# A down projection in seven products for eight, with its splits shared by GpSimd and VectorE

## The reference, cut to what matters

```python
def ffn_sublayer(x, g_pre, w_up_l, w_down_l, g_post):
    h = rmsnorm(x, g_pre)
    a = jax.nn.relu(jnp.einsum('btd,df->btf', h, w_up_l))
    return x + rmsnorm(jnp.einsum('btf,fd->btd', a * a, w_down_l), g_post)
```

## Time and profile before

| | |
|---|---|
| median of 3 runs | 2623.96 us (2621.02 to 2625.25) |
| span of the profiled execution | 2616.5 us |
| PE busy | 2570.5 us, 98% |
| POOL busy | 1296.8 us, 50% |
| ACT busy | 934.8 us, 36% |
| DVE busy | 761.8 us, 29% |

### The profile page before, as it was taken

The page is one execution under the profiler, slowest core; times in us unless marked ns, Lnnn a source line. Parts: engine busy times, 40 slices in busy tenths (PEclk is TensorE's granted clock), DMA queues, the critical chain, the costliest instruction groups (busy, mean ns, idle before and its releaser), DMA issues.

```text
span 2616.5 us, 34806 instructions
## 1 busy us (share of the span) xinstructions
PE 2570.5 (98%) x13946; PEld 2226.2 (85%) x13946; DVE 761.8 (29%) x1667; ACT 934.8 (36%) x1594; POOL 1296.8 (50%) x832
## 2 busy tenths in 40 slices
PE   7999999999999999999999999999999999999998
PEld 6899999999996467788888888878888878898997
DVE  6431111266663225311112111232111234112114
ACT  4001110087775534432234223253323244332232
POOL 1210000067762565855556567476567365654553
PEclk9999999999999999999999999999999999999999
DMA  5312314289977954543345354355454253532332
GB/s 185 113 41 67 109 59 121 69 174 191 172 141 205 297 172 153 193 145 129 113 145 194 129 173 145 112 178 176 149 175 145 98 178 126 171 130 92 131 129 89
DMA packets 264105, 373.72 MB, mean 143 GB/s; under 512 B 78677, under 2 KB 199069, under 8 KB 259033
## 3 DMA queue, kind: packets, MB, share of 16 engines
q1 hardware_dynamic: 243410, 263.37, 35.4%
q10 hardware_dynamic: 14518, 89.43, 9.5%
q0 software_dynamic: 6016, 18.68, 2.5%
HBM read 323.39 MB, written 103.76 MB: 163 GB/s over the span
## 4 chain that ended last, share of the span: by engine, by line
PE 91%; POOL 2%; DVE 2%; ACT 1%; issue 1%; DMA 1%; SPq 0%; ACTq 0%; DVEq 0%; POOLq 0%
PE ml_y L1911 31%; PE ml_up L1869 8%; PE ml_up L1871 8%; PE ml_up L1870 8%; PE pj_acc L481 6%; PE pj_acc L483 6%; PE pj_acc L482 6%; PE at_o L1150 5%; PE at_turn L1130 3%; PE at_score L1119 2%; PE at_score L1120 1%; PE de_s L2574 1%; POOL ml_w_lo L1784 1%; PE de_kt L2555 1%; PE ml_y L1906 1%
## 5 line engine op out<-in xcount | busy, mean ns | idle before, releaser
L1784 POOL TENSOR_TENSOR ml_w_lo<-em_raw,ml_w_hi 128x1024 fp32r<-128x1024 f32 x288 | 700.9, 2435 | 449.3 <-ACT ml_w_hi L1956 449.3
L1956 ACT CAST ml_w_hi<-em_raw 128x1024 fp32r<-128x1024 f32 x288 | 301.7, 1048 | 546.5 <-PE ml_y L1911 353.0
L1911 PE MATMUL ml_y<-ml_w_hi,ml_a_hi 128*128 128x512 f32 x1216 | 475.9, 391 | 3.3 <-POOL ml_w_lo L1784 3.3
L1911 PE MATMUL ml_y<-ml_w_hi,ml_a_lo 128*128 128x512 f32 x1216 | 473.4, 389 | 0.0
L1911 PE MATMUL ml_y<-ml_w_lo,ml_a_hi 128*128 128x512 f32 x1216 | 473.4, 389 | 0.0
L1869 PE MATMUL ml_up<-ml_h_hi,ml_w_hi 128*128 128x512 f32 (+1 forms) x1280 | 450.0, 352 | 1.9 <-POOL ml_w_lo L1784 1.9
L1871 PE MATMUL ml_up<-ml_h_hi,ml_w_lo 128*128 128x512 f32 (+1 forms) x1280 | 449.7, 351 | 0.0
L1870 PE MATMUL ml_up<-ml_h_lo,ml_w_hi 128*128 128x512 f32 (+1 forms) x1280 | 449.6, 351 | 0.0
L481 PE MATMUL pj_acc<-pj_h_hi,pj_w_hi 128*128 128x424 f32 (+1 forms) x800 | 290.0, 363 | 5.8 <-DVE pj_h_lo L699 5.8
L482 PE MATMUL pj_acc<-pj_h_lo,pj_w_hi 128*128 128x424 f32 (+1 forms) x800 | 283.2, 354 | 0.0
L483 PE MATMUL pj_acc<-pj_h_hi,pj_w_lo 128*128 128x424 f32 (+1 forms) x800 | 283.2, 354 | 0.0
(11 more groups left out here) (274 smaller groups left out, 3342.4 us busy)
## 6 DMA issues: line engine op xcount, KB each, us to landing
em_raw<-in_w_up SPq DMA_DIRECT2D x64, 1024.0 KB, 5.3
em_raw<-in_w_down SPq DMA_DIRECT2D x64, 1024.0 KB, 5.1
out_o_a_k_s<-in_cache_a_k ACTq DMA_DIRECT2D x8, 3060.0 KB, 12.6
out_o_a_v_s<-in_cache_a_v ACTq DMA_DIRECT2D x8, 3060.0 KB, 12.1
em_raw<-scratch_pt SPq DMA_DIRECT2D x34, 512.0 KB, 7.0
em_raw<-in_w_out SPq DMA_DIRECT2D x16, 1024.0 KB, 5.0
scratch_pt<-pj_proj SPq DMA_DIRECT2D x10, 1056.0 KB, 4.1
pj_w<-in_w_in SPq DMA_DIRECT2D x20, 512.0 KB, 3.9
```

The costliest lines, as they stand in the source:

```text
L1784: nc.gpsimd.tensor_tensor(split_of(w_lo, n), raw_of(n), f32(split_of(w_hi, n)), ALU.subtract).then_inc(w_lo_ready, 1)
L1911: last = pe.matmul(out, p[:, f, t0:t0 + m], w[:, b, :], start=(f == 0 and p is act_hi and w is hi), stop=(f == PF - 1 and p is act_lo))
L1956: nc.scalar.copy(split_of(w_hi, n), raw_of(n)).then_inc(w_hi_ready, 1)
```

## The change

**Seven products for eight.** The hidden blocks of a part are now four (`PARTS` is 8, not 4), and a part's down projection is seen as a product of 2x2 blocks: the rows are the token tiles 0, 1 (one half, 256 tokens) and 2, 3 (the other), the inner halves are two hidden blocks each, and the columns are the two halves of D. A Strassen scheme computes it with seven products, called P1, P7, P2, P6, P5, P3, P4 in their order, in place of eight. Each has 12 matmuls (two token tiles, two inner blocks, three per product). Sums of activations (`first_sums`, `second_sums`: four per part, L2403) and of weights (`w_sum`: four per part, in place in `em_raw`, L2448) come first, on DVE. P2 is accumulated onto the bank of P1, P3 onto P5, P4 onto P7, each after DVE has read the bank. Three products go straight to the output tile, P1 and P6 into an extra tile `ml_shared` that is added at the end of a group (`share`). The 64 samples keep the ordinary product: 16 matmuls a part in P1, P7, P2 and P3, which is as many as before.

**Who splits.** POOL keeps the `w_lo` of P1, P7, P2 and P6 and of the op units; DVE makes the `w_lo` of the up units and of P5, P3 and P4 (L2454). Of the seven `a_lo` of a part, DVE makes five (L2426), POOL two (L1922), each of 128x512.

**Order.** The first two up units of the next part stand between the products: a part is now up2, up3, P1, P7, up0 of the next, P2, P6, up1 of the next, P5, P3, P4. The last part of a group has no such up units and has the h steps instead. Chain and finish stand at `SLOTS`: up2, P1, P2, the next up1, P3, and the next up2 and up3. Every down unit now ends its banks, so DVE adds after each of them (L2480, L2482). Groups alternate between the tiles `em_hx` and `em_y`. The end of the program is written out by hand for DVE in `close()`, and POOL has taken the products with the gain there.

```diff
+    PARTS = 8
...
+    H_AT = (0, 1, 2, 3, 4)
+    LEADS = (1, 3)
...
+    P1, P7, P2, P6, P5, P3, P4 = range(7)
+    PRODUCTS = 7
+    ONTO = {P2: P1, P3: P5, P4: P7}
+    SLOT = (0, 1, 2, 3, 4, 5, 7)
+    KEPT = 6
+    SAMPLE_SLOT = {P1: 0, P2: 2, P3: 4, P7: 6}
+    LO_BY_POOL = (P1, P7, P2, P6)
+    BY_DVE, BY_POOL = (P1, P7, P2, P6, P5), (P3, P4)
...
+                for i in range(DF if part else 0, PF):
                     yield "up", g, part, i
-                for i in range(DOWNS):
+                for i in range(PRODUCTS):
                     yield "down", g, part, i
-                    if part == LAST - 1 and g in (1, 2):
-                        if i == PD and len(tiles(g + 1)) > PROMPT_TILES:
...
+    BANK, BEFORE = {}, {}
+    latest, held = {b: -1 for b in range(Y_BANKS)}, {}
+    for step in UNITS:
+        kind, g, part, i = step
+        for j in sums_of(step):
+            q = sum_at(step, j)
+            if kind == "down" and i in ONTO and j < PAIRS:
+                bank = held.pop((g, part, ONTO[i], j))
+            else:
+                bank = min((b for b in latest if b not in held.values()), key=lambda b: latest[b])
+                if kind == "down" and i in ONTO.values() and j < PAIRS:
+                    held[g, part, i, j] = bank
+            BANK[q], BEFORE[q] = bank, latest[bank]
+            latest[bank] = q
+
...
+    SLOTS = (("up", 0, 2), ("down", 0, P1), ("down", 0, P2), ("up", 1, 1), ("down", 0, P3), ("up", 1, 2), ("up", 1, 3))
...
+        def wait_load_spent(engine, load):
+
+            kind, g, part, i = LOADS[load]
+            if kind != "down":
+                wait_lo(engine, UNIT_OF[kind, g, part, i + 1])
+            elif i == 0:
+                wait_lo(engine, UNIT_OF["down", g, part, P6])
+                engine.wait_ge(w_summed, 4 * (g * PARTS + part) + 4)
+            else:
+                wait_lo(engine, UNIT_OF["down", g, part, P4])
+
         def raw_of(n):
...
             def split_lo(n):
+                if n >= NU or lo_by_dve(n):
+                    return
                 pool.wait_ge(w_hi_ready, n + 1)
                 nc.gpsimd.tensor_tensor(split_of(w_lo, n), raw_of(n), f32(split_of(w_hi, n)),
                                         ALU.subtract).then_inc(w_lo_ready, 1)
 
...
+            def low(at, his, slot, frm):
+                pool.wait_ge(a_hi_done, 7 * at + his)
+                nc.gpsimd.tensor_tensor(a_lo[:, slot, :], frm, f32(a_hi[:, slot, 0:2 * HT]), ALU.subtract).then_inc(a_lo_done, 1)
...
+                split_lo(n + AHEAD)
+                if kind == "up" and i == DF and has_samples(g):
+                    low_samples(part, 0)
+                if kind == "down" and i == P1 and has_samples(g):
+                    low_samples(part, 1)
+                if kind == "down" and i == P2:
+                    low(at, 6, SLOT[P3], a_raw[:, SLOT[P3], :])
+                    low(at, 7, SLOT[P4], a_raw[:, SLOT[P4], :])
...
+            def wait_operand(step):
+                kind, g, part, i = step
+                at = part_of(step)
+                if i in BY_DVE:
+                    pe.wait_ge(a_lo_by_dve, 5 * at + BY_DVE.index(i) + 1)
+                else:
+                    pe.wait_ge(a_lo_done, 2 * at + BY_POOL.index(i) + 1)
...
-                if k0 == PD - 1:
+                    out = y_ps[BANK[q]][:, :]
+                    for f in range(DF):
+                        c = f * HT + j * P
+                        for p, w in ((a_hi, hi), (a_hi, lo), (a_lo, hi)):
+                            last = pe.matmul(out, p[:, SLOT[i], c:c + P], w[:, f, :],
+                                             start=(i not in ONTO and f == 0 and p is a_hi and w is hi),
+                                             stop=(f == DF - 1 and p is a_lo), skip_group_check=i in ONTO)
...
+                if kind == "down" and i in (P7, P6, P5, P4):
+                    act.wait_ge(w_summed, 4 * part_of(step) + (P7, P6, P5, P4).index(i) + 1)
+                else:
+                    wait_loaded(act, load_of(step))
...
+                    if kind == "down" and i == P1:
+                        act.wait_ge(emptied, turns_through(("up", g, part, PF - 1)))
+                        high(SLOT[P2], kept_raw)
+                        if has_samples(g):
+                            act.wait_ge(sample_summed, part + 1)
+                            high_samples(part, 1)
+                        act.wait_ge(a_summed, 4 * at + 3)
+                        high(SLOT[P6], a_raw[:, SLOT[P6], :])
+                    if kind == "down" and i == P7:
+                        high(SLOT[P5], a_raw[:, SLOT[P5], :])
+                        act.wait_ge(a_summed, 4 * at + 4)
+                        high(SLOT[P3], a_raw[:, SLOT[P3], :])
+                    if kind == "down" and i == P2:
+                        high(SLOT[P4], a_raw[:, SLOT[P4], :])
...
+            def second_sums(step):
+                kind, g, part, i = step
+                at = part_of(step)
+                by_f = [a_raw[:, s, :].rearrange("p (f t) -> p f t", t=HT) for s in range(DBLK)]
+                dve.wait_ge(emptied, turns_through(step))
+                a_sum(by_f[SLOT[P5]], a[:, 1, :, :], by_f[SLOT[P4]], ALU.add)
+                dve.wait_ge(a_summed, 4 * at + 2)
+                a_sum(by_f[SLOT[P6]], by_f[SLOT[P5]], a[:, 0, :, :], ALU.subtract)
+                dve.wait_ge(a_summed, 4 * at + 3)
+                a_sum(by_f[SLOT[P3]], by_f[KEPT], by_f[SLOT[P6]], ALU.subtract)
...
+                    wait_loaded(dve, LOAD_OF["down", g, part, 1])
+                    to, one, other, op = right[:, top], right[:, bottom], right[:, top], ALU.subtract
+                if which == P6:
+                    wait_loaded(dve, LOAD_OF["down", g, part, 0])
+                    wait_lo(dve, UNIT_OF["down", g, part, P1])
+                    dve.wait_ge(w_summed, 4 * part_of(step) + 1)
+                    to, one, other, op = left[:, top], right[:, top], left[:, top], ALU.add
+                if which == P5:
+                    wait_lo(dve, UNIT_OF["down", g, part, P7])
+                    dve.wait_ge(w_summed, 4 * part_of(step) + 2)
+                    to, one, other, op = right[:, top], right[:, bottom], left[:, top], ALU.subtract
+                if which == P4:
+                    wait_lo(dve, UNIT_OF["down", g, part, P5])
+                    to, one, other, op = right[:, top], left[:, bottom], left[:, top], ALU.subtract
+                nc.vector.tensor_tensor(to, one, other, op).then_inc(w_summed, 1)
+
...
+                    if not closing:
+                        split_lo(n + AHEAD)
+                        if n + AHEAD < NU and UNITS[n + AHEAD][0] == "down" and UNITS[n + AHEAD][3] == P3:
+                            w_sum(UNITS[n + AHEAD], P4)
                     if kind == "up":
+                        if g and part == 0 and i == 0:
+                            share(g - 1)
+                        if i == DF:
+                            first_sums(step)
+                            w_sum(step, P7)
+                            low(at, 1, SLOT[P1], a[:, 0, :, :].rearrange("p f t -> p (f t)"))
+                            low(at, 2, SLOT[P7], a_raw[:, SLOT[P7], :])
+                        if i == PF - 1:
+                            w_sum(step, P6)
+                            w_sum(step, P5)
                         hidden(step)
-                    elif tiles_of(step) and step != UNITS[-1]:
-                        add_y(step)
+                        if i == PF - 1:
+                            second_sums(step)
+                            low(at, 3, SLOT[P2], kept_raw)
+                    elif kind == "op" and sums_of(step):
+                        add_op(step)
+                    elif kind == "down" and not closing:
+                        for j in sums_of(step):
+                            add_down(step, j)
+                        if i == P1:
+                            low(at, 4, SLOT[P6], a_raw[:, SLOT[P6], :])
+                            low(at, 5, SLOT[P5], a_raw[:, SLOT[P5], :])
+                    n += 1```

**DVE, parts 0 to 3 of group 0, before.** These rows show the adds to the output tile (L2194, L2196) and the squares (L2161), with `ml_y` the result banks and `ml_up` the banks of the up products.

```order
L2194 COPY em_y<-ml_y 128x512 x8
L2161 SCALAR_TENSOR_TENSOR ml_a<-ml_up,ml_r 128x512 x8
L2196 TENSOR_TENSOR em_y<-ml_y,em_y 128x512 x8
L2161 SCALAR_TENSOR_TENSOR ml_a<-ml_up,ml_r 128x512 x8
L2196 TENSOR_TENSOR em_y<-ml_y,em_y 128x512 x8
L2161 SCALAR_TENSOR_TENSOR ml_a<-ml_up,ml_r 128x512 x8
```

646 lines of the change are left out of this document (422 added, 224 removed).

## The result

The changed kernel takes 2742.95 us (median of 4 runs, 2739.21 to 2750.83) against 2624.61 for the one before on the same chip: a ratio of 1.0452, 95% interval 1.0432 to 1.0473. It is 118 us slower where 36 were forecast. Its profiled execution took 2740.59 us, with a span of 2738.8.

A forecast was written before the change was run, and what follows sets the result against it. PE's matmuls, one behind the other, were taken to bound the kernel. Waits of 127 us, less 3.6 of old waits and 87.1 of removed matmuls, net +36.3: span 2652.8, time 2660 us; range 2580 to 2700, the forecast's own 2630 to 2685.

The forecast's parts named there:

- P5 to P3: P3 goes onto P5's bank and waits for DVE's add: 0.95 us in 21 parts, 20 us.
- later slots: P2, next up1, P3, next up2 and up3: DVE's chores cost 4 us per chain, 1 per finish, 15 us.
- first slots: At up2 of a chain or finish, norm, scaling and residual delay DVE's list: 4.5 us in six places, 25.5 us in all.
- second slots: At P1, P2's `w_lo` waits behind POOL's residual: 3.8 us in a chain, 3.0 in a finish, 19 us in all.
- last parts: Last part of groups 0 to 2: second h waits 4.8 us, P3 2.7 us; 22.5 us in all.
- closing part: The part with samples and `close()` instead of h steps: P3 waits behind P5 about 6 us.
- merges: Four pairs in groups 1 and 2: POOL's combine precedes DVE's sums at up3 and up0, 3.3 us a pair, 13 us.
- transposes and conv: In part 5 of groups 1 and 2: 2 us of waits each, 4 us.
- The collision on the port: POOL operations and DVE operations with two SBUF inputs hold each other off: 7 us in all over the first slots.
- the clock falls: Rival: 20 long waits each slow one unit of 5.44 us to the lower clock, 109 us, time 2769; chance 0.02.
- The tail: After the last matmul, 7.9 us before; two tiles wait with three scalings of two halves: 2 us more.
- The 7.5 us "around the span": Added to the forecast span of 2652.8 us to get the time, as the amount by which time exceeds span.

The follow-up runs named there:

- run 6: The changed kernel with all weight splits of the MLP's down products on VectorE, none on GpSimd: 2697.93 us.
- run 10: Changed kernel with the edits of run 6 and Run 7, P5's first add before P4's split, and activation splits and residuals on VectorE too: 2658.38 us.
- run 2: The kernel before, with 56 short pauses: in parts 1 and 2 TensorE waits ahead of up units for the previous unit's relu: 2676.32 us.
- Run 7: The changed kernel with another closing order, prompt tiles' first halves squared and multiplied by the gain before the samples': 2735.38 us.

## Why the prediction was wrong

- **Removed matmuls.** Right: 384 fewer, and the page counts 13562; intervals 0.2276 us for 0.2270.
- **PE's waits.** Right in sum: forecast 125 without the closing's 2, 121 net of the old 3.6; measured +124.7. (The 3.6 are from 1150 us on the earlier trace rows, not the whole stretch, which had 7.6 from the op units' first product.) By terms, forecast and measured: P5 to P3 in the 14 undisturbed parts 13.3 and 12.3; later slots with the other seven P3 21.7 and 32.7; first slots (P7 and up0) in five places 22.5 and 20.4; second slots 17.4 and 17.3; last parts 22.5 and 25.6; both slots in group 3 4.5 and 6.7; closing part 6 and 6.3; merges 13 and 7.6; transposes and conv 4 and nothing; the 3 us left lie in the op units. That the sum is so near is partly luck: the later slots are 11 us too low, the merges and transposes 9 too high. A plain part lasted 42.1 us for 41.8.
- **The collision on the port.** Right as a mechanism: 1625 ns for a sum of weights of 1.22, 1216 ns for a split of activations put at 0.65. Its price, 7 us, was not tested by itself: run 6 gave 45 and run 10 another 12, but both also shorten POOL's queue. Rows 7 don't show POOL beside an add out of PSUM; the closing rows above do, and the add keeps its time.
- **The clock: the step that failed.** The sum has no term for it, and the rival "the clock falls" got a chance of 0.02, since "the rows around 945 us speak against it". Those 4.2 us are four waits of 0.56 to 1.51 us, far from the forecast's own stalls of 3 to 5. And even they kept the clock by luck of that execution: in six of the 14 traces the same code lost it between 941 and 946 us. So in run 2, ahead of its pauses:

```profile
930.00:960.00 30.00, 25.84 (x121) 18.17 (x118) 8.28 (x18) 11.26 (x20) 21.01 (x25) 0.90 0.44 141
```

  The first row, with one wait of 2.68 us and a clock of 0.88, was the one that resembled the forecast's stalls, some twenty of them. The rival's price was wrong too, 109 us: a spell costs some 1 to 3 us, not a whole unit of 5.44. The runs showed 189 intervals at the lower clock and 38.6 us in its place.
- **A first matmul after a wait** starts 0.16 us late, and the other single intervals over 0.30 us have grown from 39 to 106: no term of the sum, 15.0 us together.
- **The tail** was priced at 2 us more and took 16.8. The forecast counted scalings and not that POOL's five products by the gain would be released together, beside DVE's last adds. Run 7 gives 4.3 us of it; where the other 12 go (two tiles' sums and five scalings after the last matmul, in turn with POOL) was read and not tested.
- **The stretch ahead of the MLP** was 8.1 us longer in this one execution, which is not the change's doing.
- **The 7.5 us "around the span"** are a misreading that does no harm to the sum: in every execution with both figures the time is 1.7 to 2.7 us above the span; the other 5 or 6 us are that the profiled execution of the kernel before was a fast one.

Without the clock's 39 us the time would be about 2704 and still above the range of 2580 to 2700, so the tail and the restarts count too.

Of the prediction's own marks most came true: DVE 1700 us, waits above 85 us, the places. Before up0 PE waited only 1.2 to 2.8 us where 3 to 5 were named, with 1.2 to 2.5 more before P7. The first mark failed, that PE's starts stay 0.227 us apart, and it is the one that catches the clock; the line drawn for being wrong (waits under 85 us) left it out.

## What to carry to other kernels

A stall on TensorE isn't priced by its length alone: behind every stop of 2.85 us and more, and behind about half of those from 1.5 to 2.8, matmuls at the lower clock cost some 1 to 3 us more here. Where such waits can't be taken away, matmuls that nobody reads, sized to the wait, gave back 18.5 us here. Don't share SBUF-to-SBUF work between VectorE and GpSimd by counting idle time: moving four splits a part back to the busier engine was worth 45 us, the port and GpSimd's queue together. And an edit that removes 87 us of matmuls from a kernel at 98% TensorE must leave the other engines room in every part, not on average: at 62% busy, VectorE was late in every part of groups 0 to 2. In group 3, where the samples make a part longer, PE did not wait from 2372 to 2687 us.

## What the hardware showed beyond that

- Stops of 3.06 us were followed in twelve cases of twelve by 6 to 13 slow intervals, most of 0.43 us; 42 stops of 0.73 us, one every 6.4 us, by none; four of 2.45 us in two cases.
- The same code ahead of the op units, with three or four stops of at most 1.6 us in some 9 us, lost the full clock there in six profiled executions of 14.
- Operations on GpSimd that follow each other without a gap held VectorE off together: five of 1.2 to 1.3 us made an add of 0.68 us last 6.58. The Trainium skill ("SBUF — State Buffer", Who interferes with whom) has the loser wait for one whole instruction; here it waited for all five (6.58 us beside their 6.17).
- The same code ahead of the MLP took up to 8.1 us longer in one profiled execution than in another.
